# Modulation by VectorE multiply-and-sum in a two-layer hybrid backbone: shift and scale of the first layer in the filter stage, the rest beside the short convolutions

## The chip, the cores and the metric

One core of a Trainium2 chip runs the whole program. The metric is the device time of one execution in microseconds (us), the median of several runs. Engines are named as in the profile: TensorE (PE, weight loads PEld), VectorE (DVE), ScalarE (ACT), GpSimd (POOL) and SyncE (SP), which here only issues DMAs. Each engine works through its own instructions in order and waits on semaphores; a DMA is issued by an engine's queue, and an issue that stands behind a wait comes after it.

## The reference

Two layers are applied to 128 context tokens and 1024 latent tokens (1152 columns in all), 1024 channels wide. What the change touches is the modulation; it depends on the conditioning vectors alone (one for the context tokens, one for the latent tokens):

```python
mod = jax.nn.silu(cond) @ p['w_ada'] + p['b_ada']
shift, scale, gate = jnp.split(mod[:, None, :], 3, axis=-1)
h = rms_norm(x, p['norm_g']) * (1.0 + scale) + shift
proj = h @ p['w_in']
# three branches: long convolution (Hyena), differential attention, pooling
out = merged @ p['w_out']
return x + gate * out, kv
```

`w_ada` is 1024 x 3072 a layer, f32. Before the layers the spectra of the Hyena filters are computed: a small sine network gives filter taps, they are multiplied by a decay, normalised, and transformed.

## The kernel before

All tensors lie with channels on the 128 partitions; 1024 channels are KD = 8 tiles. Products of f32 numbers are made of three matmuls with operands split into a rounded high part and a rest, so each weight tile goes through ScalarE (rounding, `high`) and GpSimd or VectorE (the rest, `low`).

`filters` (phase "fspec", the first 566 us) has a head and four units. In the head TensorE runs the sine network (lines 434 and 451; VectorE reduces the angles in `reduce_and_sin`, lines 221 to 226; ScalarE takes the sine, line 714; VectorE makes the remainder of the last hidden layer, line 566), SP copies the hidden layer to the other partitions (lines 380 and 384), and for each of CT = 4 channel tiles and two directions TensorE makes the taps (`hidden_to_taps`, line 467) and VectorE multiplies them by the decay (`decayed`, line 578). GpSimd adds and subtracts directions (`both_of`, lines 695 and 696), VectorE folds (line 597), TensorE turns the folds (`turn`, line 486), ScalarE and VectorE split them (lines 747 and 605). ScalarE also squares x (line 727), GpSimd sums the squares (line 703) and TensorE sums over channels (line 526). Then four units (layer x order) of NS = 17 steps each: at a step SP stores the last spectrum tile (`store_spectrum`, lines 351 to 356; lines 353 and 354 are two stores of one tile) and loads the transform matrix of two steps later (`load_matrix`, line 339), ScalarE rounds that matrix (`matrix_high`, line 758) and copies the spectrum out (line 764), VectorE makes the matrix's rest (`matrix_low`, line 625), TensorE multiplies (line 514). In the same steps the taps of the next unit are made.

The modulation of both layers stands in `filters`, too. 48 tiles (24 a layer) of `w_ada`, 512 KB each, are loaded by SP into three buffers (`load_ada`, line 344) and multiplied on TensorE (`modulation`, line 443: KD matmuls of 128x128 weights by two columns a tile): five tiles in the sine network, eight before the taps, eight between the turns, seven in each unit from step 6 on. VectorE adds the bias (line 633).

Then a loop over the layers: `keys_values`, `attention`, `mixers_in`, `long_conv`, `branches_out`, `output`. `mixers_in` (phase "mixin") projects 28 tiles (`proj`, line 1292). SP loads the weight of tile t+2 in its step t (`load_w`, line 1224; from tile 3 on, and two buffers). ScalarE's order in step t is: round the weight of tile t+2 (`high`, line 1330), evict tile t (lines 1339 to 1341), issue two table copies. GpSimd makes the weight's rest (line 1399). For the first T_PL = 12 tiles VectorE runs the short convolution (lines 1416 to 1426), and SP stores it one step later, from tile 4 on (`store_conv`, lines 1240 and 1241). Four pooling tiles and twelve gating tiles follow. The next lines are SP's and ScalarE's loops before:

```python
for t in range(T_END):                       # SP
    if 3 <= t + 2 < T_END:
        load_w(t + 2) if t >= 1 else None
    ...
    if CT <= t - 1 < T_PL:
        store_conv(t - 1)
for t in range(T_END):                       # ScalarE
    if t + 2 < T_END:
        high(t + 2)
    if t < T_PL:
        evict_hy(t)
```

## Time and profile before

| | us |
|---|---|
| median of three runs | 3848.51 (3844.27 to 3859.57) |
| the profiled execution's own time | 3852.03 |
| its span in the trace | 3850.1 |
| TensorE busy in the span | 3500.3 |
| VectorE / ScalarE / GpSimd busy | 1654.7 / 1106.5 / 795.7 |
| mean granted TensorE clock | 0.941 of full |

A busy TensorE is not one at its peak: matmuls are pipelined and their ends are modelled. The rows below are instructions or groups of them with their line in the kernel; "idle" is the time that the engine stood still before, with what ended it.

### The profile page before, as it was taken

How to read it: one execution, taken by the hardware profiler on the slowest of the kernel's cores; microseconds unless marked ns; L12 is line 12 of the kernel's file. 1: busy time of each engine (PE TensorE's matmuls, PEld its weight loads, DVE VectorE, ACT ScalarE, POOL GpSimd, SP SyncE). 2: the span in 40 equal slices, each digit the busy share in tenths (PEclk: the TensorE clock that was granted, in tenths of full speed). 3: DMA queues.
4: the chain of work that ended last, by engine and by line, in shares of the span. 5: the costliest groups of instructions: out<-in, count | busy, mean ns of one | idle time of the engine just before them, and what ended most of it. 6: DMA issues, size and time to landing. Idle time of an engine off the chain costs nothing. (4 is left out here: it accounts for less than half of the span.)

```text
span 3850.1 us, 49480 instructions
## 1 busy us (share of the span) xinstructions
PE 3500.3 (91%) x19198; PEld 3255.1 (85%) x19198; DVE 1654.7 (43%) x2065; ACT 1106.5 (29%) x1765; POOL 795.7 (21%) x393
## 2 busy tenths in 40 slices
PE   5889888989999999988888889999999999888889
PEld 5777768988998999986788879889888999866889
DVE  2344524254454334237734132444544342377351
ACT  1233424243344312112211142334443112122111
POOL 2222202122122111112212322121221111122123
PEclk7688989999999999999999989999999999989999
DMA  5455553332332245346543433322322454456334
GB/s 173 149 176 178 164 194 124 123 84 68 82 85 63 83 151 185 139 160 206 194 152 119 163 142 125 86 62 79 91 63 77 142 185 142 156 199 218 134 119 168
DMA packets 212192, 520.14 MB, mean 135 GB/s; under 512 B 37012, under 2 KB 84757, under 8 KB 210614
## 3 DMA queue, kind: packets, MB, share of 16 engines
q1 hardware_dynamic: 203030, 458.56, 36.0%
q10 hardware_dynamic: 8960, 58.73, 5.0%
q8 instruction: 146, 2.39, 0.3%
q14 instruction: 56, 0.46, 0.0%
HBM read 381.19 MB, written 163.07 MB: 141 GB/s over the span
## 5 line engine op out<-in xcount | busy, mean ns | idle before, releaser
L2053 PE MATMUL ps<-hh,w_high 128*128 128x384 f32 x1152 | 413.2, 359 | 5.5 <-ACT attn_fout L2204 4.4
L2053 PE MATMUL ps<-hh,w_low 128*128 128x384 f32 x1152 | 393.9, 342 | 0.0
L2053 PE MATMUL ps<-hl,w_high 128*128 128x384 f32 x1152 | 392.4, 341 | 0.0
L1292 PE MATMUL ps<-hh,w_high 128*128 128x384 f32 x1344 | 310.7, 339 | 7.2 <-PEq L116 7.2
L1292 PE MATMUL ps<-hl,w_high 128*128 128x384 f32 x1344 | 306.7, 336 | 0.0
L1292 PE MATMUL ps<-hh,w_low 128*128 128x384 f32 x1344 | 306.4, 335 | 0.0
L2363 DVE TENSOR_REDUCE attn_nmax<-ps 128x1 f32<-128x1280 f32 x144 | 195.4, 1357 | 145.6 <-PE ps L2076 145.5
L1292 PEld LDWEIGHTS ps<-hh,w_high 128*128 128x128 f32 x1344 | 240.3, 189 | 11.6 <-POOLq L1396 7.8
L2230 ACT ACTIVATE low<-ps,attn_nmax 128x1280 f32<-128x1280 f32 x144 | 176.3, 1224 | 236.6 <-DVE attn_nmax L2363 236.6
L2383 DVE TENSOR_TENSOR attn_wl<-ps,attn_wh 128x512 fp32r<-128x512 f32 (+2 forms) x200 | 117.4, 587 | 290.1 <-ACT attn_wh L2240 290.1
L1292 PEld LDWEIGHTS ps<-hl,w_high 128*128 128x128 f32 x1344 | 240.9, 189 | 0.0
L1292 PEld LDWEIGHTS ps<-hh,w_low 128*128 128x128 f32 x1344 | 240.8, 189 | 0.0
L2053 PEld LDWEIGHTS ps<-hh,w_high 128*128 128x128 f32 x1152 | 222.2, 193 | 11.5 <-ACT attn_fout L2204 9.2
L2053 PEld LDWEIGHTS ps<-hl,w_high 128*128 128x128 f32 x1152 | 222.0, 193 | 0.0
L2053 PEld LDWEIGHTS ps<-hh,w_low 128*128 128x128 f32 x1152 | 220.9, 192 | 0.0
L2300 POOL TENSOR_TENSOR w_low<-w_raw,w_high 128x1024 fp32r<-128x1024 f32 x48 | 119.0, 2480 | 475.2 <-ACT w_high L2197 475.2
L2509 PE MATMUL ps<-hh,branch_wh 128*128 128x384 f32 x576 | 138.1, 349 | 41.9 <-POOL branch_wl L2552 41.9
L1737 POOL TENSOR_TENSOR conv_prod<-conv_prod 128x512 f32<-128x512 f32 x64 | 100.8, 1595 | 313.3 <-DVE conv_prod L1746 313.3
L1456 DVE TENSOR_TENSOR mixin_zg<-mixin_zg,mixin_yin 128x1152 f32<-128x1152 f32 x24 | 55.6, 2318 | 227.3 <-ACT mixin_zg L1358 227.3
L443 PEld LDWEIGHTS ps<-fspec_scond,fspec_araw 128*128 128x128 f32 x768 | 122.5, 249 | 35.4 <-DMA fspec_araw<-in_w_ada 31.5
L443 PE MATMUL ps<-fspec_scond,fspec_araw 128*128 128x2 f32 x768 | 119.4, 288 | 31.3 <-DMA fspec_araw<-in_w_ada 31.3
L2509 PEld LDWEIGHTS ps<-hh,branch_wh 128*128 128x128 f32 x576 | 106.4, 196 | 46.9 <-POOL branch_wl L2552 46.9
(289 smaller groups left out, 7548.8 us busy)
## 6 DMA issues: line engine op xcount, KB each, us to landing
tables<-in_dft_conv ACTq DMA_DIRECT2D x64, 512.0 KB, 4.4
gates<-attn_fout SPq DMA_DIRECT2D x144, 192.0 KB, 2.0
branch_gate<-gates SPq DMA_DIRECT2D x48, 576.0 KB, 3.9
H_dram<-fspec_hout SPq DMA_DIRECT2D x100, 256.0 KB
fspec_araw<-in_w_ada SPq DMA_DIRECT2D x48, 512.0 KB, 4.2
w_raw<-in_w_mg ACTq DMA_DIRECT2D x48, 512.0 KB, 3.9
conv_dh<-tables SPq DMA_DIRECT2D x96, 256.0 KB, 2.9
conv_dl<-tables SPq DMA_DIRECT2D x96, 256.0 KB, 3.6
```

Source lines behind the costliest of these rows:

```text
L443: last = pe.matmul(ps[:, 5, 2 * i:2 * i + 2], araw[:, i % 3, k, :], scond[:, k, :], start=(k == 0), stop=(k == KD - 1))
L1292: last = pe.matmul(dst, w[:, b, k, :], x[:, k, cols], start=(k == 0 and n == 0), stop=(k == KD - 1 and n == 2))
L1456: dve.tensor_tensor(zg[:, i % 2], zg[:, i % 2], yin[:, i % 2], ALU.mult).then_inc(S["gated"], 1)
L1737: pool.tensor_tensor(prod[:, p % 2, 2 * b], prod[:, p % 2, 2 * b], prod[:, p % 2, 2 * b + 1], (ALU.subtract, ALU.add)[b]).then_inc(S["gp"], 1)
L2053: last = pe.matmul(ps[:, X_BANK, 0:CH], w[:, j % 2, k, :], x[:, k, (c % 3) * CH:(c % 3 + 1) * CH], start=(k == 0 and n == 0), stop=(k == K ...
L2230: nc.scalar.activation(dst[:, 0:n], flat[:, 1536 * c:1536 * c + n], ACT.Exp, bias=nmax[:, c:c + 1], accum_out=total[:, u % 2, c:c + 1]).th ...
L2300: pool.tensor_tensor(fwl[:, b], fraw[:], fwh[:, b].bitcast(F32), ALU.subtract).then_inc(S["flo"], 1)
L2363: dve.tensor_reduce(nmax[:, c:c + 1], flat[:, 1536 * c:1536 * c + n], AX_X, ALU.max, negate=True).then_inc(S["max"], 1)
L2383: dve.tensor_tensor(weights(wl, u, at, cnt), ps[:, T_BANK, 0:cnt * P].rearrange("p (k c) -> p k c", c=P), weights(wh, u, at, cnt).bitcast( ...
L2509: last = pe.matmul(dst, w[:, b, k, :], x[:, q, cols], start=(k == 0 and n == 0), stop=(k == CT - 1 and n == 2))
```

## The change

TensorE's matmuls for the modulation go, with the bias loads of `filters`. `w_ada` is laid out by rows of output channels (128 partitions x 1024), and the conditioning vectors, after the Silu, are spread over all partitions. One output tile is then two VectorE instructions (`tensor_tensor_reduce`, one per vector): multiply 1024 elements by the vector and sum along the row. The 16 tiles of shift and scale of the first layer run in the head of `filters`; their loads (`w_ada_first`) are spread over SP's queue there. The other 24 of each layer's pass (the gate of this layer, shift and scale of the next) run in `mixers_in`, two behind each short convolution, with two load buffers that are the pooling's later. The bias is added where the values are used. The spread vectors are stored to DRAM once (`cond_kept`) and loaded back in `mixers_in`.

x's tiles are loaded earlier, six at once and two when a buffer is free, each with its own semaphore; ScalarE squares each on arrival, between the sines, and GpSimd's sums go into the first. The second store of a spectrum tile (line 354) goes; the first then counts for both.

```diff
@@ filters, SyncE
                 def load_ada(i):
                     if i >= 3:
-                        sp.wait_ge(S["a_used"], i - 2)
-                    sp.dma_start(araw[:, i % 3], A["w_ada"][i // 24, i % 24]).then_inc(s_ain[i % 3], 16)
+                        sp.wait_ge(S["ada"], 2 * (i - 2))
+                    sp.dma_start(araw[:, i % 3], A["w_ada_first"][i]).then_inc(s_ain[i % 3], 16)
+                def load_x(k):
+                    if k >= 6:
+                        sp.wait_ge(S["xadd"], k - 5)
+                    sp.dma_start(xs[k], A["x"][:, k]).then_inc(s_xin[k], 16)
...
-                        sp.dma_start(H_dram[l, o, t // 2, :, 0, :], src).then_inc(sem, 16)
-                        sp.dma_start(H_dram[l, o, t // 2, :, 2, :], src).then_inc(sem, 16)
+                        sp.dma_start(H_dram[l, o, t // 2, :, 0, :], src).then_inc(sem, 32)
...
-                sp.dma_start(cond[:], A["cond"]).then_inc(S["cond"], 16)
-                for i in range(3):
+                sp.dma_start(condb, A["cond"].to_broadcast([P, 2, D_MODEL])).then_inc(S["cond"], 16)
+                for i in range(2):
                     load_ada(i)
+                for k in range(6):
+                    load_x(k)
+                load_ada(2)
...
+                sp.wait_ge(S["scond"], 1)
+                sp.dma_start(cond_kept, condb).then_inc(S["cst"], 16)
+                for k in range(6, KD):
+                    load_x(k)
+                for i in range(3, 5):
                     load_ada(i)
...
-                for i in range(9, 14):
+                for i in range(5, 9):
                     load_ada(i)
                 for u in range(2, CT):
                     load_decay(u)
-                for i in range(14, ADA_AHEAD):
+                    for i in range(9 + 2 * (u - 2), 11 + 2 * (u - 2)):
+                        load_ada(i)
+                for i in range(13, NA):
                     load_ada(i)
@@ filters, TensorE
-                def modulation(i):
...
-                        last = pe.matmul(ps[:, 5, 2 * i:2 * i + 2], araw[:, i % 3, k, :], scond[:, k, :],
-                                         start=(k == 0), stop=(k == KD - 1))
...
+                pe.wait_ge(S["xadd"], KD - 1)
+                for i in range(NT // P):
+                    last = pe.matmul(ps[:, 5, i:i + 1], xs[0][:, i * P:(i + 1) * P], ones[:, 0:1], start=True, stop=True)
+                last.then_inc(S["ssm"], 1)
                 pe.wait_ge(S["dup"], 96)
@@ filters, VectorE
+                def modulation(i):
+                    if i == 0:
+                        dve.wait_ge(S["scond"], 1)
+                    dve.wait_ge(s_ain[i % 3], 16 * (i // 3) + 16)
+                    for st in range(2):
+                        if 2 * i + st:
+                            dve.wait_ge(S["ada"], 2 * i + st)
+                        dve.tensor_tensor_reduce(waste, araw[:, i % 3], condb[:, st], 1.0, 0.0, ALU.mult, ALU.add,
+                                                 modn[:, i, st:st + 1]).then_inc(S["ada"], 1)
+                for i in range(2):
+                    modulation(i)
                 dve.wait_ge(S["pre"], 2)
...
+                for i in range(2, 6):
+                    modulation(i)
                 for m in range(2):
                     matrix_low(m)
                 for ct in range(CT):
                     for d in range(2):
                         decayed(0, ct, d)
+                        modulation(6 + 2 * ct + d)
+                for i in range(14, NA):
+                    modulation(i)
@@ filters, GpSimd and ScalarE
                     if u == CT - 1:
-                        pool.wait_ge(S["ssm"], 1)
+                        pool.wait_ge(S["ada"], 2 * NA)
+                        pool.wait_ge(S["cst"], 16)
...
+                squares((0, 1))
                 for i in range(2):
+                    if i == 1:
+                        squares((2, 3, 4))
                     act.wait_ge(S["ang"], i + 1)
                     nc.scalar.activation((h1, h2)[i], ang, ACT.Sin).then_inc(S["sin"], 1)
...
+                squares((5, 6, 7))
...
+                    if m == 0:
+                        act.wait_ge(S["ada"], 2 * NA)
...
-                            act.wait_ge(S["a_used"], min(NA, ADA_AHEAD + ADA * n))
+                            if n:
+                                act.wait_ge(S["hpst"], 16 * n)
@@ keys_values, VectorE
-                chain(dve.tensor_copy(mod[:], mods[:, bass.ds(l, 1)].rearrange("p a m n -> p (a m) n")))
                 dve.wait_ge(S["par"], 16)
+                for st in range(2):
+                    chain(dve.tensor_tensor(mod[:, 0:2 * KD, st], modn[:, :, st], pr("b_ada")[:, 0:2 * KD], ALU.add))
@@ mixers_in, SyncE
+                def load_ada(i):
+                    if i >= 2:
+                        sp.wait_ge(S["ada"], 2 * (i - 1))
+                    sp.dma_start(araw[:, i % 2], A["w_ada"][l, i]).then_inc(s_ain[i % 2], 16)
                 load_w(2)
+                sp.dma_start(condb, cond_kept).then_inc(S["cond"], 16)
+                for i in range(2):
+                    load_ada(i)
...
                 for t in range(T_END):
                     if 3 <= t + 2 < T_END:
                         load_w(t + 2) if t >= 1 else None
+                    for i in (2 * t + 2, 2 * t + 3):
+                        if i < NA:
+                            load_ada(i)
@@ mixers_in, ScalarE and VectorE
                 def pool_out(g):
                     act.wait_ge(S["pmm"], 2 * g + 1)
+                    if g == 0:
+                        act.wait_ge(S["ada"], 2 * NA)
...
+                def modulation(i):
...
+                    for st in range(2):
...
+                        dst = mod[:, 2 * KD + i, st:st + 1] if i < KD else modn[:, i - KD, st:st + 1]
+                        dve.tensor_tensor_reduce(waste, araw[:, i % 2], condb[:, st], 1.0, 0.0, ALU.mult, ALU.add, dst
+                                                 ).then_inc(S["ada"], 1)
...
+                    for i in (2 * t, 2 * t + 1):
+                        modulation(i)
+                dve.wait_ge(S["ada"], 2 * NA)
+                for st in range(2):
+                    at = mod[:, 2 * KD:3 * KD, st]
+                    dve.tensor_tensor(at, at, pr("b_ada")[:, 2 * KD:3 * KD], ALU.add).then_inc(S["bada"], 1)
```

## Rows read from the trace of the kernel before

**Rows 1.** Page: TensorE's busy time; two groups (count | busy, mean ns | idle).

```profile
PE 3500.3 (91%) x19198; PEld 3255.1 (85%) x19198; DVE 1654.7 (43%) x2065; ACT 1106.5 (29%) x1765; POOL 795.7 (21%) x393
...
L2363 DVE TENSOR_REDUCE attn_nmax<-ps 128x1 f32<-128x1280 f32 x144 | 195.4, 1357 | 145.6 <-PE ps L2076 145.5
...
L443 PE MATMUL ps<-fspec_scond,fspec_araw 128*128 128x2 f32 x768 | 119.4, 288 | 31.3 <-DMA fspec_araw<-in_w_ada 31.3
```

**Rows 2.** Windows of line 443 alone: stretch, length, PE, PEld, clock, DMA share, GB/s.

```profile
122.00:167.00 45.00, 27.38 (x128) 27.67 (x128) 0.50 0.61 206
...
167.00:565.00 398.00, 50.00 (x432) 52.81 (x432) 0.90 0.52 171
```

**Rows 3.** Timeline of ScalarE, last unit: start, duration, instruction [idle before, ended by].

```profile
506.13 0.62 ACT L758 CAST fspec_dh<-fspec_draw 128x512 fp32r<-128x512 f32 x1 [2.88 <-DMA fspec_draw<-in_dft_taps]
...
514.15 0.62 ACT L758 CAST fspec_dh<-fspec_draw 128x512 fp32r<-128x512 f32 x1 [6.42 <-DMA fspec_draw<-in_dft_taps]
...
547.65 0.62 ACT L758 CAST fspec_dh<-fspec_draw 128x512 fp32r<-128x512 f32 x1 [3.83 <-DMA fspec_draw<-in_dft_taps]
...
551.95 0.62 ACT L758 CAST fspec_dh<-fspec_draw 128x512 fp32r<-128x512 f32 x1 [3.20 <-DMA fspec_draw<-in_dft_taps]
...
556.88 0.62 ACT L758 CAST fspec_dh<-fspec_draw 128x512 fp32r<-128x512 f32 x1 [3.83 <-DMA fspec_draw<-in_dft_taps]
```

**Rows 4.** Timeline of SyncE's queue, last unit.

```profile
503.70 1.34 SPq L344 DMA_DIRECT2D fspec_araw<-in_w_ada  x3
```

**Rows 5.** Timeline of ScalarE in `mixers_in` of the first layer.

```profile
1357.09 1.05 ACT L1330 CAST w_high<-w_raw 128x1024 fp32r<-128x1024 f32 x1 [10.29 <-PE ps L1292]
...
1358.99 0.28 ACT L1341 COPY aux<-ps 128x128 f32<-128x128 f32 x1
1369.57 1.05 ACT L1330 CAST w_high<-mixin_raw 128x1024 fp32r<-128x1024 f32 x1 [10.30 <-PE ps L1292]
```

**Rows 6.** Timelines of the head, all engines; last row VectorE in the first unit.

```profile
48.02 1.48 DVE L221 TENSOR_SCALAR fspec_both<-ps,fspec_fpar 128x1152 f32<-128x1152 f32 x1 [26.54 <-PE ps L451]
...
56.09 1.16 ACT L714 ACTIVATE fspec_both<-fspec_both 128x1152 f32<-128x1152 f32 x1 [33.41 <-DVE fspec_both L226]
...
60.67 1.36 DVE L566 TENSOR_TENSOR fspec_h2l<-fspec_both,fspec_h2h 128x1152 fp32r<-128x1152 f32 x1
61.58 11.48 POOL L703 TENSOR_TENSOR fspec_both<-fspec_both,fspec_taps 128x1152 f32<-128x1152 f32 x4 [61.12 <-ACT fspec_taps L727]
...
68.36 5.25 DVE L625 TENSOR_TENSOR fspec_dl<-fspec_draw,fspec_dh 128x512 fp32r<-128x512 f32 x2 [6.33 <-ACT fspec_dh L758]
...
70.18 0.60 SPq L384 DMA_DIRECT2D fspec_h2l<-fspec_h2l  x1
...
92.31 1.36 DVE L578 TENSOR_TENSOR fspec_taps<-ps,fspec_decay 128x1152 f32<-128x1152 f32 x1 [18.70 <-PE ps L467]
...
169.38 0.69 DVE L625 TENSOR_TENSOR fspec_dl<-fspec_draw,fspec_dh 128x512 fp32r<-128x512 f32 x1 [4.95 <-ACT fspec_dh L758]
```

**Rows 7.** Timeline of TensorE: last turn of the head, first spectrum.

```profile
158.59 1.95 PE L486 MATMUL ps<-ident,fspec_fold 128*128 128x128 f32 x8
...
162.82 2.07 PE L511 MATMUL ps<-fspec_mid,fspec_sgn 1*128 1x512 f32 x2 [0.78 <-DVE fspec_mid L610]
```

**Rows 8.** Timeline of VectorE in `mixers_in`: a convolution's end; a 128x1024 operation.

```profile
1363.93 0.35 DVE L1422 SCALAR_TENSOR_TENSOR low<-aux,mixin_cw 128x128 f32<-128x128 f32 x1
...
1594.32 1.21 DVE L1865 TENSOR_TENSOR aux<-low 128x1024 f32<-128x1024 f32 x1
```

**Rows 9.** Line 1224, the weight loads of `mixers_in`: time from issue to landing.

```profile
DMA to landing us min/median/max: 3.5/4.1/6.8
```

**Rows 10.** Timeline of SyncE's queue in `mixers_in`: a convolution's store, the next weight load.

```profile
1401.62 0.35 SPq L1240 DMA_DIRECT2D mix<-aux  x1
...
1402.63 0.65 SPq L1224 DMA_DIRECT2D mixin_raw<-in_w_mix  x1
```

**Rows 11.** Timeline of GpSimd in `mixers_in`.

```profile
1358.22 2.40 POOL L1399 TENSOR_TENSOR w_low<-w_raw,w_high 128x1024 fp32r<-128x1024 f32 x1 [10.07 <-ACT w_high L1330]
```

More of the change, by code:

```diff
@@ L198, in build @@
                     with nc.sbuf_tensor("w_raw1", [P, KD, P], F32) as raw1:
-                        keys_values(nc, A, O, l, ps, par, pr, mods, mod, ident, ones, sums, x_state, hh, hl, low, qraw, kraw,
+                        keys_values(nc, A, O, l, ps, par, pr, modn, mod, ident, ones, sums, x_state, hh, hl, low, qraw, kraw,
                                     craw, (fraw, raw1), fwh, fwl, lam, gain, qk, vrows)
@@ L301, in even_groups @@
             return [(j // 3, 2 * (j % 3)) for j in range(GA) if 9 + j // 2 == s]
-        def modulations(n, s):
-            i = ADA_AHEAD + n * ADA + s - 6
-            return [i] if 6 <= s < 6 + ADA and i < NA else []
         def odd_groups(s):
@@ L404, in _ @@
                             load_matrix(m + 2)
-                        if s == 4:
-                            sp.wait_ge(S["hpst"], 16 * (n + 1))
-                        for i in range(NA):
-                            if (s == 4 and i in sum((modulations(n, q) for q in (6, 7, 8)), [])) or (
-                                    s >= 6 and i in modulations(n, s + 3)):
-                                load_ada(i)
                         if n + 1 < NU and s in (3, 5, 7, 9):
@@ L523, in _ @@
                         hidden_to_taps(0, ct, d)
-                pe.wait_ge(S["xadd"], KD - 1)
-                for i in range(NT // P):
-                    last = pe.matmul(ps[:, 5, 128 + i:129 + i], xs[-1][:, i * P:(i + 1) * P], ones[:, 0:1], start=True,
-                                     stop=True)
-                last.then_inc(S["ssm"], 1)
                 for ct in range(CT):
-                    for i in (13 + 2 * ct, 14 + 2 * ct):
-                        modulation(i)
                     for f in (0, 2, 4):
@@ L538, in _ @@
                             prompt_spectrum(n)
-                        for i in modulations(n, s):
-                            modulation(i)
                         for ct, f in odd_groups(s):
@@ L792, in _, with keys_values @@
                                 high_part(n + 1, ct, f)
-def keys_values(nc, A, O, l, ps, par, pr, mods, mod, ident, ones, sums, x_state, hh, hl, low, qraw, kraw, craw, raws,
+def keys_values(nc, A, O, l, ps, par, pr, modn, mod, ident, ones, sums, x_state, hh, hl, low, qraw, kraw, craw, raws,
                 fwh, fwl, lam, gain, qk, vrows):
@@ L1179, with mixers_in @@
 T_PL, T_Z, T_END = 12, 16, 28
-def mixers_in(nc, A, l, ps, pr, hh, hl, v, aux, fold, fraw, fwh, fwl, mix, tables):
+def mixers_in(nc, A, l, ps, pr, mod, modn, cond_kept, hh, hl, v, aux, fold, fraw, fwh, fwl, mix, tables):
     with phase(nc, "mixin") as ph:
@@ L1200, in mixers_in @@
                  "pst0", "pst1", "y0", "y1", "gated", "zst0", "zst1", "dve", "tab",
-                 "fold")
+                 "fold", "cond", "ain0", "ain1", "ada", "bada")
         S = {n: ph.sem(n) for n in names}
@@ L2845, in lay_out @@
     A["w_out"] = _tiles(I["w_out"])
-    A["w_ada"] = _tiles(I["w_ada"])
-    A["cond"] = np.stack([I["c_ctx"], I["c"][0]]).reshape(2, KD, P).transpose(2, 1, 0)
+    ada = I["w_ada"].transpose(0, 2, 1).reshape(DEPTH, 3 * KD, P, D_MODEL)
+    A["w_ada_first"] = ada[0, 0:2 * KD]
+    A["w_ada"] = np.stack([np.concatenate([ada[l, 2 * KD:], ada[min(l + 1, DEPTH - 1), 0:2 * KD]]) for l in range(DEPTH)])
+    A["cond"] = np.stack([I["c_ctx"], I["c"][0]])[None]
     conv = np.concatenate([I["hy_conv_w"], I["hy_conv_b"][:, None]], axis=1)
```

87 lines of the change are left out of this document (38 added, 49 removed).

## The prediction

> **What bounds the kernel now.** Read the page first: TensorE is called busy for 91% of the span [rows 1], which invites the thought that any matmul taken off it is time gained. The modulation's 768 matmuls (line 443) stand there with 119.4 us busy and 31.3 us of idle time before them, which ended with a weight load. The windows of line 443 alone show where they lie: 27.4 us at half clock (0.50) in the stretch 122 to 167 us, 50.0 us in the four spectrum units from 167 to 565 us [rows 2]; the rest lies before 122 us. So nothing after 565 us can win. Three stretches decide, each with its own bound.
>
> The spectrum units are not bound by TensorE. Before each rounding of a transform matrix ScalarE is waiting for the matrix's DMA; near the end, where no modulation is left, the roundings still come 4.30 and 4.93 us apart by turns [rows 3]. That is a loop: rounding, spectrum copied out (the next instruction on ScalarE), store and next load on SP's queue, landing. The longer turn is the one with two stores. Where three ada tiles of 512 KB are issued at 503.70 [rows 4], the loop takes 8.02 us (506.13 to 514.15, idle until the DMA) [rows 3]: the tiles delay the matrix behind them.
>
> The head of the filter stage is a chain through all engines; its matmuls wait for ada DMAs. In `mixers_in`, where the new work goes, TensorE is the bound: ScalarE's weight rounding at line 1330 follows TensorE, 12.48 us a tile (1357.09 to 1369.57) [rows 5].
>
> **The change part by part.**
>
> *Head, to the first tap.* Now: the second angle is ready at 56.0, its remainder ends at 62.0 (60.67 + 1.36), the first taps start at 92.31, the first spectrum at 162.82 [rows 6, 7]. The wait for ada tiles ahead of the second layer's matmuls goes. New on that path: two squarings before the first sine (they wait for x 0 and 1, queued behind 2 MB of cond and ada, so about 1 to 2 us late), then four VectorE multiply-sums. No row shows such an instruction. The nearest is a plain 128x1024 two-input operation, 1.21 us [rows 8], 1.24 with a semaphore between; I take 1.24. Below that nothing is likely, since it reads the same elements; above, a multiply and a separate sum would be 1.21 + 1024/1280 x 1.36 (the reduction's row [rows 1]) = 2.3. Four take 5 us, beside the second layer's matmuls; the second reduction takes 8.1 (48.02 to 56.09) [rows 6]. GpSimd's sums of x squared (four in 11.48) move from after this chain into it. That costs: two VectorE splits that take 0.69 each at other times took 5.25 together beside these sums [rows 6]. With two or three sums of 2.87 in the way the second angle comes at 42 (36 without, 45 with all), the remainder at 48: 14 us earlier.
>
> Behind it SP copies the hidden layer as now (last copy issued at 70.18, 8 us after the remainder [rows 6], landing later), then loads ada tile 5, on which VectorE waits with the matrix splits and the first taps queued behind; and the three last sums, the x sums on TensorE and six multiply-sums share that time. I put the first taps at 68 against 92.3: 24 us gained.
>
> *Head, taps to spectrum.* Now 70.5 us (92.31 to 162.82). Then: eight taps of 1.36 with two multiply-sums each are 30.7; four multiply-sums more, 5.0; GpSimd's six fold sums in between hold VectorE up by about 12; the last fold sums wait for all multiply-sums (their buffer holds cond) and cost up to 5.3 beside VectorE's folds; then four groups of folds and turns without the two modulations each, 5.0 a group (0.8 for a fold, 4.2 from the turn at 158.59 to the spectrum at 162.82 [rows 7]), 20. Together 68 to 73; TensorE's 27.4 us give little, since VectorE takes their place. **Head: 27 us gained** (18 if the sums block more, 42 if they hardly block).
>
> *Spectrum units.* The gain is in the loop, not in the 50 us of matmuls. (a) The second store is dropped: 4.93 becomes 4.30, 0.63 x 8 a unit x 4 = 20. (b) The three tiles together: 8.02 becomes 4.9 with its own double store counted above, 3.4 x 4 = 14; the single tiles later about 1.5 us a unit, 6. **40 us gained**; 30 if TensorE at the lower clock sets some steps, 50 if the shorter steps also free waits for the folds.
>
> *Layer stage.* In `keys_values` a copy becomes two small additions: under 0.5 us a layer, hidden behind the load of `par`.
>
> *`mixers_in`.* 24 pairs of multiply-sums a layer, two pairs behind each of 12 short convolutions. VectorE has room: 4 x 1.24 = 5.0 in a tile of 12.48. But the 24 loads go on SP's queue, two a tile, with two buffers; the second waits for the multiply-sums of the same tile. Behind that wait stand the stores of the convolution and `load_w` of the next step (tile t+3); ScalarE waits for this weight in `high` **ahead of** the eviction of its own tile; the convolution waits for the eviction. A loop, then, priced from the start h of `high`:
> - h to evicted: 1358.99 + 0.28 - 1357.09 = 2.2 [rows 5];
> - convolution to 1363.93 + 0.35 = 1364.28: h + 7.2 [rows 5, 8];
> - multiply-sums: h + 12.2; ada issue and wake 0.5;
> - the weight: 4.1 issue to landing as median now, 3.5 to 6.8 [rows 9], and one ada tile of the same size straight ahead of it: 4.6;
> - ScalarE's wake 0.1.
>
> That is 17.4 a tile against 12.48. From the sixth on two stores go ahead (1401.62 to 1402.63, 1.0 [rows 10], and their bytes): 18.7. Eleven tiles pass through the loop: 5 x 17.4 + 6 x 18.7 = 199 against 11 x 12.48 = 137, 62 more. TensorE has 12.48 - 3.6 = 8.9 us of cover (the next but one tile needs `high` 1.05 and GpSimd's 2.40 after h [rows 5, 11]), once. **53 us lost a layer, 106 in two.** Bounds: landing 3.5 with nothing ahead gives 16.2 and 17.1, 37 a layer; 6.8 gives 19.5 and 20.4, 74 a layer. I take the middle since the ada tile is surely ahead. A lower clock after TensorE's waits hides in them.
>
> Sum: 3852.0 (profiled execution) - 27 - 40 + 106 = 3891. The median shown is 3.5 below the profiled execution: **3887.5**.
>
> *Put at nothing.* The 1 MB store of cond is issued some 17 us after the start and waited for near 110. x's loads pass ada tile 2, w3 and the decays, none of which VectorE or TensorE needs before 28 us; the last two x loads wait on GpSimd's first sums with ada 3 and 4 behind them, needed some 15 us later. ScalarE's new waits (all multiply-sums before the first spectrum copy, the prompt store before its buffer is written again) are met earlier by a stage or a unit. In `mixers_in` the pool's copy waits for all multiply-sums, done two tiles before; without that cover it would cost one eviction. The bias additions are two small instructions.
>
> *A rule against it.* Each multiply-sum reads two f32 tensors in SBUF and sums at once. The Trainium skill, "Vector Engine (DVE) Microarchitecture Reference", section 7, warns that one family of instructions that can accumulate halves its throughput with two such sources, as no port is left for the accumulator. No run here shows such a sum; the plain two-source form takes 1.21 us for 1024 elements, so some 1.2 ns an element with its fixed part [rows 8]. What a half rate would give is priced, from rows, as the second rival.
>
> **Rivals.**
> 1. *The loop is covered* (other side: faster). If weights land before TensorE needs them, only the head and the units count: 3848.5 - 67 = 3781.5. It decides where multiply-sums, issue and landing fit into 12.48 - 7.2 = 5.3 us; 5.0 + 0.5 + 4.6 = 10.1 speaks against it, as does the order in the code. For it: nothing in the rows but VectorE's idle time. A weaker form, larger gains (92) with the cheap loop (75), gives 3831.5.
> 2. *The multiply-sum takes 2.3 us*, a multiply plus a sum. In the loop 4 x 1.06 = 4.2 more a tile, 47 a layer, 94 in two; in the head some 25: 3887.5 + 119 = 4006. For it: nothing shows the fused form; against: a reduction alone also runs at an element per 1.06 ns.
> 3. *The two sides meet*: gains near 85 against losses near 85, 3848.5. The head is the weakest sum of all, its chain has five engines.
>
> **How the numbers follow.** A measurement of this kernel tells about 0.5% (19 us) from no change. Forecast with its bounds, beyond 0.5% slower: 0.60; rival 2: 0.07; rival 3, within 0.5%: 0.20; rival 1 in both forms, as far as it is beyond 0.5%: 0.13. So faster 0.13, same 0.20, slower 0.67. Range: gains 92 with losses 75 give 3831; gains 42 with losses 148 give 3954.5. Rounded, 3830 to 3960: below it lies most of rival 1, above it rival 2.
>
> **What would show it.** Right: the rows of line 1330 in `mixers_in` some 17 to 19 us apart in the first twelve tiles and 12.5 after, ended by a DMA instead of TensorE, TensorE idle before line 1292 by some 50 us a layer; the stage after the filters starting near 500 instead of 566; even and odd matrix roundings both near 4.3. Wrong: line 1330 still ended by TensorE at 12.5 (rival 1); multiply-sums of 2 us or more (rival 2); first spectrum later than 145 or earlier than 120 (the head).

## The result and the profile after

The median went from 3850.51 us (four runs) to **3911.37 us** (four runs), a ratio of 1.0166 with a 95% interval of 1.0146 to 1.0186: slower by 60.9 us. The forecast was 3887.5 us, 39 above the median then shown, within 3830 to 3960. The profiled execution took 3909.5 us, its span 3907.8.

Cut at the same instructions in both traces (first spectrum matmul, last matrix rounding, first instruction of ScalarE in each later stage), the spans compare so:

| stretch | before, us | after, us | difference | forecast |
|---|---|---|---|---|
| head, to the first spectrum | 162.82 | 134.80 | -28.0 | -27 |
| four spectrum units, to the last rounding | 394.06 | 357.57 | -36.5 | -40 |
| keys, values and attention, layer 1 | 773.4 | 775.3 | +1.9 | 0 |
| `mixers_in` and long convolution, layer 1 | 575.2 | 638.0 | **+62.8** | +53 |
| `mixers_in` and long convolution, layer 2 | 576.6 | 637.3 | **+60.7** | +53 |
| everything else | 1368.0 | 1364.8 | -3.2 | 0 |
| span | 3850.1 | 3907.8 | +57.7 | +39 |

The long convolution is not where it lies: in the first layer the last roundings of `mixers_in` stand 61 us further from its first one than before (1267.67 to 1663.24 against 1330.25 to 1664.53).

The timeline of ScalarE in `mixers_in` of the first layer, after (start, duration, instruction, idle before and what ended it). These rows answer [rows 5]; line 1330 is now line 1347:

```profile
1336.18 1.05 ACT L1347 CAST w_high<-w_raw 128x1024 fp32r<-128x1024 f32 x1 [16.08 <-DMA w_raw<-in_w_mix]
...
1338.09 0.28 ACT L1358 COPY aux<-ps 128x128 f32<-128x128 f32 x1
1353.46 1.05 ACT L1347 CAST w_high<-mixin_raw 128x1024 fp32r<-128x1024 f32 x1 [15.10 <-DMA mixin_raw<-in_w_mix]
...
1370.41 1.05 ACT L1347 CAST w_high<-w_raw 128x1024 fp32r<-128x1024 f32 x1 [14.76 <-DMA w_raw<-in_w_mix]
...
1389.67 1.05 ACT L1347 CAST w_high<-mixin_raw 128x1024 fp32r<-128x1024 f32 x1 [17.08 <-DMA mixin_raw<-in_w_mix]
...
1409.32 1.05 ACT L1347 CAST w_high<-w_raw 128x1024 fp32r<-128x1024 f32 x1 [17.46 <-DMA w_raw<-in_w_mix]
```

A rounding that TensorE used to end every 12.48 us is ended by the weight's DMA, first some 17.5 us apart and later 19 to 20. VectorE, and SyncE's queue, in the same tiles (x2: two issues in the time given, with the wait between them):

```profile
1338.40 1.86 DVE L1447 TENSOR_SCALAR aux<-aux,mixin_cw 128x1154 f32<-128x1154 f32 x1 [8.27 <-ACT aux L1358]
...
1342.95 0.35 DVE L1453 SCALAR_TENSOR_TENSOR low<-aux,mixin_cw 128x128 f32<-128x128 f32 x1
1343.22 1.22 DVE L1437 CUSTOM_DVE_ANT_0 mixin_diff<-mixin_grow,mixin_pout 128x1024 f32<-128x1024 f32 x1
...
1347.12 1.23 DVE L1437 CUSTOM_DVE_ANT_0 mixin_diff<-mixin_grow,mixin_pout 128x1024 f32<-128x1024 f32 x1
```

```profile
1345.88 2.98 SPq L1260 DMA_DIRECT2D mixin_grow<-in_w_ada  x2
1349.04 0.33 SPq L1230 DMA_DIRECT2D mixin_raw<-in_w_mix  x1
...
1399.24 2.98 SPq L1260 DMA_DIRECT2D mixin_grow<-in_w_ada  x2
1402.27 1.13 SPq L1246 DMA_DIRECT2D mix<-aux  x1
1403.44 0.43 SPq L1247 DMA_DIRECT2D mix<-aux  x1
1404.06 0.81 SPq L1230 DMA_DIRECT2D w_raw<-in_w_mix  x1
```

Read across the three: eviction ends at 1338.37, the convolution at 1343.30, the fourth multiply-sum at 1348.35, and 0.7 us later the weight is issued whose landing lets ScalarE go on at 1353.46. From the sixth tile on the two stores lie between the last ada issue and the weight.

What TensorE loses to it, in two groups of all instructions (count | busy, mean ns | idle before), and what a multiply-sum costs (the profile calls it a custom instruction) in `mixers_in` and in the head:

```profile
L1309 PE MATMUL ps<-hh,w_high 128*128 128x384 f32 x1344 | 326.5, 352 | 91.0 <-POOL w_low L1418 83.8
...
L1437 DVE CUSTOM_DVE_ANT_0 mixin_diff<-mixin_grow,mixin_pout 128x1024 f32<-128x1024 f32 x96 | 117.5, 1224 | 5.1
...
L544 DVE CUSTOM_DVE_ANT_0 fspec_hout<-fspec_araw,fspec_both 128x1024 f32<-128x1024 f32 x32 | 58.7, 1835 | 3.2 <-DMA fspec_araw<-in_w_ada_first 1.9
```

The projection (line 1309, before 1292) now stands idle for 83.8 us until the weight's rest is there, and its three groups are busy for 960.4 us instead of 923.8: 120 us together, close to the 123.5 us that both layers lose. The head, in VectorE's and then TensorE's timeline, answers [rows 6, 7]; the roundings of the last unit answer [rows 3]:

```profile
26.23 3.48 DVE L544 CUSTOM_DVE_ANT_0 fspec_hout<-fspec_araw,fspec_both 128x1024 f32<-128x1024 f32 x1
...
41.35 0.76 DVE L227 TENSOR_SCALAR fspec_both<-fspec_both 128x1152 f32<-128x1152 f32 x1
...
46.73 3.69 DVE L559 TENSOR_TENSOR fspec_h2l<-fspec_both,fspec_h2h 128x1152 fp32r<-128x1152 f32 x1
...
68.33 1.35 DVE L571 TENSOR_TENSOR fspec_taps<-ps,fspec_decay 128x1152 f32<-128x1152 f32 x1
```

```profile
134.80 2.07 PE L497 MATMUL ps<-fspec_mid,fspec_sgn 1*128 1x512 f32 x2 [0.77 <-DVE fspec_mid L603]
```

```profile
483.69 0.62 ACT L757 CAST fspec_dh<-fspec_draw 128x512 fp32r<-128x512 f32 x1 [3.21 <-DMA fspec_draw<-in_dft_taps]
488.08 0.62 ACT L757 CAST fspec_dh<-fspec_draw 128x512 fp32r<-128x512 f32 x1 [3.29 <-DMA fspec_draw<-in_dft_taps]
492.37 0.62 ACT L757 CAST fspec_dh<-fspec_draw 128x512 fp32r<-128x512 f32 x1 [3.18 <-DMA fspec_draw<-in_dft_taps]
```

### The profile page after: what moved, and what is told of

It is laid out like the page before. It is cut to its first block and busy times, and to the rows that moved or that the text cites. A ratio compares the mean times of both kernels' runs of the same rounds, so it can differ in the third digit from the quotient of the medians.

```text
span 3907.8 us, 48339 instructions
## 1 busy us (share of the span) xinstructions
PE 3423.0 (88%) x18430; PEld 3170.0 (81%) x18430; DVE 1835.4 (47%) x2323; ACT 1109.0 (28%) x1765; POOL 805.0 (21%) x393
## 5 line engine op out<-in xcount | busy, mean ns | idle before, releaser
L2090 PE MATMUL ps<-hh,w_high 128*128 128x384 f32 x1152 | 414.6, 360 | 5.5 <-ACT attn_fout L2241 4.4
L1309 PE MATMUL ps<-hh,w_high 128*128 128x384 f32 x1344 | 326.5, 352 | 91.0 <-POOL w_low L1418 83.8
L2090 PE MATMUL ps<-hh,w_low 128*128 128x384 f32 x1152 | 395.0, 343 | 0.0
L2090 PE MATMUL ps<-hl,w_high 128*128 128x384 f32 x1152 | 393.6, 342 | 0.0
L1309 PEld LDWEIGHTS ps<-hh,w_high 128*128 128x128 f32 x1344 | 250.2, 197 | 101.8 <-POOL w_low L1418 90.2
L1309 PE MATMUL ps<-hl,w_high 128*128 128x384 f32 x1344 | 318.2, 346 | 0.0
L1309 PE MATMUL ps<-hh,w_low 128*128 128x384 f32 x1344 | 315.7, 343 | 0.0
L1309 PEld LDWEIGHTS ps<-hl,w_high 128*128 128x128 f32 x1344 | 251.9, 197 | 0.0
L1309 PEld LDWEIGHTS ps<-hh,w_low 128*128 128x128 f32 x1344 | 250.2, 196 | 0.0
L2090 PEld LDWEIGHTS ps<-hh,w_high 128*128 128x128 f32 x1152 | 222.7, 193 | 11.7 <-ACT attn_fout L2241 9.2
L2090 PEld LDWEIGHTS ps<-hl,w_high 128*128 128x128 f32 x1152 | 223.0, 194 | 0.0
L2090 PEld LDWEIGHTS ps<-hh,w_low 128*128 128x128 f32 x1152 | 221.8, 193 | 0.0
L1447 DVE TENSOR_SCALAR aux<-aux,mixin_cw 128x1154 f32<-128x1154 f32 x24 | 44.8, 1868 | 216.3 <-ACT aux L1358 216.3
L2241 ACT ACTIVATE attn_fout<-ps 128x384 f32<-128x384 f32 x144 | 71.0, 493 | 256.6 <-PE ps L2090 256.6
```

Source lines behind the costliest of these rows:

```text
L1309: last = pe.matmul(dst, w[:, b, k, :], x[:, k, cols], start=(k == 0 and n == 0), stop=(k == KD - 1 and n == 2))
L1447: chain(dve.tensor_scalar(dst, u[:, b, 1:1 + n], taps[:, 1:2], taps[:, 3:4], ALU.mult, ALU.add))
L2090: last = pe.matmul(ps[:, X_BANK, 0:CH], w[:, j % 2, k, :], x[:, k, (c % 3) * CH:(c % 3 + 1) * CH], start=(k == 0 and n == 0), stop=(k == K ...
L2241: nc.scalar.activation(fout[:, c % 2], ps[:, X_BANK, 0:CH], ACT.Tanh, scale=0.5).then_inc(S["fev"], 1)
```

## The experiments

The theory on record: the weight load in `mixers_in` stands on SyncE's queue behind a wait for the multiply-sums, and ScalarE's order closes that into a loop; the units gain what leaves their loop on the same queue, not TensorE's work; the head gains by the waits for ada tiles. Where one run is given (no interval), the verdict rests on its trace: stretches that an edit does not touch differ by up to 9 us from one execution to the next (the four units took 352.1 to 361.1 us in the changed kernel and the six variants of it that leave them alone).

**Is it the queue's order?** In `mixers_in` of the changed kernel:

```diff
 for t in range(T_END):                       # SP
-    if 3 <= t + 2 < T_END:
-        load_w(t + 2) if t >= 1 else None
+    if t + 3 < T_END:
+        load_w(t + 3)
     for i in (2 * t + 2, 2 * t + 3):
         if i < NA:
             load_ada(i)
```

> The changed kernel with one order turned round on SyncE's queue in mixers_in: at step t the weight of tile t+3 is issued ahead of the two ada tiles instead of behind them; same instructions, same loads. Theory (the weight load stands behind a wait for the multiply-sums, a loop of 17.4 to 20 us): the weight roundings in the first twelve tiles come 12.5 us apart and end with TensorE, the layer stage gets back 61 us a layer, 3911 - 122 = 3789 us, 62 below the kernel before. Rival A (the multiply-sums or the added traffic themselves stretch the tiles): roundings stay 16 us or more apart, 3890 to 3911. Rival B (another wait takes the place, the ada tiles land too late for VectorE and the evictions wait for it): roundings 13 to 15 us apart, 3810 to 3860.

Measured: 3813.25 us against 3847.09 for the kernel before, ratio 0.991 (0.9886 to 0.9933): 98 us back by an order alone, but not 122. ScalarE's timeline shows where the rest is, and VectorE's and SyncE's show why:

```profile
1354.67 1.05 ACT L1347 CAST w_high<-mixin_raw 128x1024 fp32r<-128x1024 f32 x1 [10.29 <-PE ps L1309]
1367.15 1.06 ACT L1347 CAST w_high<-w_raw 128x1024 fp32r<-128x1024 f32 x1 [10.29 <-PE ps L1309]
...
1380.92 1.06 ACT L1347 CAST w_high<-mixin_raw 128x1024 fp32r<-128x1024 f32 x1 [11.58 <-DMA mixin_raw<-in_w_mix]
...
1397.98 1.06 ACT L1347 CAST w_high<-w_raw 128x1024 fp32r<-128x1024 f32 x1 [14.87 <-DMA w_raw<-in_w_mix]
```

```profile
1351.84 2.98 SPq L1260 DMA_DIRECT2D mixin_grow<-in_w_ada  x2
1354.86 0.43 SPq L1246 DMA_DIRECT2D mix<-aux  x1
```

```profile
1363.01 0.88 DVE L1447 TENSOR_SCALAR aux<-aux,mixin_cw 128x1154 f32<-128x1154 f32 x1 [8.70 <-DMA mix<-aux]
```

Seven steps of 12.48 us, ended by TensorE: the first loop is gone. Then the convolution of tile 6 waits 8.7 us for the store of tile 4 (each convolution from the seventh on needs the store of two tiles back to have landed), and that store was issued at 1354.86, behind the two ada tiles, that is behind the multiply-sums of tile 5. A **second loop through the same queue**, 17 us a tile, which the first had covered. From there on one VectorE instruction a tile also runs beside GpSimd's rest of a weight and takes 3.2 to 3.6 us instead of 1.2 to 1.4 (the convolution's last one, 1382.13 to 1385.67). My expectation had not seen this loop; rival B's time (3810 to 3860) holds, but not its steps (13 to 15), and the wait that took the place is the store's and not an ada tile's.

**Another link of the same loop cut**, SyncE's order as in the changed kernel:

```diff
 for t in range(T_END):                       # ScalarE
+    if t < T_PL:
+        evict_hy(t)
     if t + 2 < T_END:
         high(t + 2)
     if t < T_PL:
-        evict_hy(t)
+        pass
```

> The changed kernel with another link of the same loop cut, SyncE's order left as it is: in mixers_in ScalarE evicts tile t of the first twelve before it rounds the weight of tile t+2. Theory: the convolution no longer waits for a weight; the weight of t+3 is issued 10.5 us after the eviction of t, lands 4.6 later, is split 3.6 later, 18.8 in all against some 23 until TensorE needs it: roundings 12.5 us apart, 3789 to 3810 us. Rival A (traffic or VectorE's work): roundings stay 16 us or more apart, 3890 to 3911.

```profile
1366.30 0.88 DVE L1449 TENSOR_SCALAR aux<-aux,mixin_cw 128x1154 f32<-128x1154 f32 x1 [6.22 <-DMA mix<-aux]
```

Measured: 3837.80 us, one run. Roundings 12.1 to 13.0 us apart from the third to the seventh (1303.30, 1315.82, 1328.27, 1340.38, 1353.37), then 14 to 18.5, where the convolution waits for a store. The same two pictures as in e1, by a cut elsewhere: the first loop needs ScalarE's order as much as SyncE's. The time expected was missed through the second loop in the main. A layer's stretch with `mixers_in` is still 10 us longer than in e1 (599.1 and 600.8 us against 588.6 and 591.8): here the weight stays behind the multiply-sums, the roundings wait for it from the third on, and the step ahead of that takes 16.6 us; the rest of the 10 was not followed up.

**More work in the loop**, each multiply-sum of `mixers_in` twice (the counts in the waits for them are doubled too):

```diff
-                    for st in range(2):
-                        if 2 * i + st:
-                            dve.wait_ge(S["ada"], 2 * i + st)
+                    for r in range(4):
+                        st = r % 2
+                        if 4 * i + r:
+                            dve.wait_ge(S["ada"], 4 * i + r)
...
```

> The changed kernel with each multiply-sum of mixers_in done twice into the same place (four more of 1.24 us a tile, 5.0). Theory: every link of the loop adds to it, so the roundings come 22.4 us apart in the first six tiles and 24.4 after, 11 x 5.0 = 55 us a layer more, 4021 us. Rival A (the traffic sets the step): the added VectorE work fits into its idle time, under 20 us more.

```profile
1366.05 1.05 ACT L1347 CAST w_high<-mixin_raw 128x1024 fp32r<-128x1024 f32 x1 [19.86 <-DMA mixin_raw<-in_w_mix]
1388.45 1.05 ACT L1347 CAST w_high<-w_raw 128x1024 fp32r<-128x1024 f32 x1 [20.21 <-DMA w_raw<-in_w_mix]
1412.70 1.05 ACT L1347 CAST w_high<-mixin_raw 128x1024 fp32r<-128x1024 f32 x1 [22.07 <-DMA mixin_raw<-in_w_mix]
```

Measured: 4012.68 us. The first five steps of the loop mean 22.3 us (17.5 in the changed kernel), the next six 24.5 (19.5): 4.8 and 5.0 us for 5.0 us of added work. VectorE's work counts in full while it stands in the loop, though in the changed kernel VectorE is idle for 7 to 10 us of each of these steps. The time is 101 us above the changed kernel's (110 expected; the rival allowed 20).

**Both loops cut.** As e1, and the stores go ahead of the ada tiles too:

```diff
+    if CT <= t - 1 < T_PL:
+        store_conv(t - 1)
     for i in (2 * t + 2, 2 * t + 3):
         ...
-    if CT <= t - 1 < T_PL:
-        store_conv(t - 1)
```

> As e1, and in mixers_in the two stores of convolution t-1 are issued ahead of the ada tiles of step t as well. In e1 the first seven tiles came 12.48 us apart and the next five about 17, where VectorE waits 5.9 to 8.7 us for the store of the convolution two tiles back, which stood behind the wait for the multiply-sums. Theory (a second loop through the same queue, hidden in the changed kernel behind the first): all roundings in mixers_in 12.5 us apart and ended by TensorE, 14 us a layer less than e1, 3813 - 28 = 3785 us, as much as the filter stage alone gains (64.5). Rival (from the sixth tile on traffic, not order, sets the step): steps of 16 to 17 stay, 3805 to 3815.

```profile
1366.48 1.05 ACT L1347 CAST w_high<-w_raw 128x1024 fp32r<-128x1024 f32 x1 [10.30 <-PE ps L1309]
1378.96 1.05 ACT L1347 CAST w_high<-mixin_raw 128x1024 fp32r<-128x1024 f32 x1 [10.30 <-PE ps L1309]
```

```profile
1363.65 3.00 SPq L1260 DMA_DIRECT2D mixin_grow<-in_w_ada  x2
1366.83 0.33 SPq L1230 DMA_DIRECT2D mixin_raw<-in_w_mix  x1
1367.20 0.68 SPq L1246 DMA_DIRECT2D mix<-aux  x1
```

Measured: **3783.04 us** against 3852.81, ratio 0.9822 (0.9806 to 0.9838). The first fourteen steps behind the first one are 12.48 us each, as in the kernel before; the two stretches with `mixers_in` take 576.2 us each, as in the kernel before (575.2 and 576.6). So the 96 multiply-sums and 48 ada loads cost nothing there: the whole loss was the order of issues on one queue.

**The units: stores, loads or matmuls?** Three edits of the kernel before. One store instead of two:

```diff
-                        sp.dma_start(H_dram[l, o, t // 2, :, 0, :], src).then_inc(sem, 16)
-                        sp.dma_start(H_dram[l, o, t // 2, :, 2, :], src).then_inc(sem, 16)
+                        sp.dma_start(H_dram[l, o, t // 2, :, 0, :], src).then_inc(sem, 32)
```

> The kernel before with the second store of a spectrum tile left away and nothing else changed. Theory (the store stands in the loop from rounding to rounding): even and odd roundings both 4.3 us apart where they were 4.30 and 4.93, the four units 20 us shorter, 3827 us. Rival (the second store is hidden by TensorE or by the next landing): within 5 us of the kernel before.

```profile
525.36 0.62 ACT L757 CAST fspec_dh<-fspec_draw 128x512 fp32r<-128x512 f32 x1 [3.20 <-DMA fspec_draw<-in_dft_taps]
529.55 0.62 ACT L757 CAST fspec_dh<-fspec_draw 128x512 fp32r<-128x512 f32 x1 [3.08 <-DMA fspec_draw<-in_dft_taps]
533.80 0.62 ACT L757 CAST fspec_dh<-fspec_draw 128x512 fp32r<-128x512 f32 x1 [3.15 <-DMA fspec_draw<-in_dft_taps]
```

Measured: 3825.33 us against 3852.81, ratio 0.9934 (0.9917 to 0.9951). Even and odd steps alike; the units 371.8 us (533.80 - 162.02) instead of 394.1, 22.3 less. The loads left out, 27 in SyncE's loop over the steps, and TensorE's wait for them (it waits for the prompt spectrum's copy instead):

```diff
-                        for i in range(NA):
-                            if (s == 4 and i in sum((modulations(n, q) for q in (6, 7, 8)), [])) or (
-                                    s >= 6 and i in modulations(n, s + 3)):
-                                load_ada(i)
...
-                    pe.wait_ge(s_ain[i % 3], 16 * (i // 3) + 16)
+                    if i < ADA_AHEAD:
+                        pe.wait_ge(s_ain[i % 3], 16 * (i // 3) + 16)
...
                         for i in modulations(n, s):
+                            pe.wait_ge(S["hpo"], n + 1)
```

> The kernel before with the 27 ada loads of the spectrum units left out; TensorE's matmuls on these tiles stay and read what lies in the buffers. Theory (the gain in the units is the loads' place on SyncE's queue, not TensorE's work): one step of 8.0 us a unit becomes 4.9, single tiles give 1.5 us a unit, 20 us in all, 3828 us. Rival (TensorE's 50 us of matmuls bound the units): no change.

Measured: units 382.4 us (542.57 - 160.22), 11.7 less, not much above the scatter of such stretches; the single run took 3835.26. The step with three tiles went from 8.4 us (196.29 to 204.68, three ada issues at 195.09) to 4.9 (193.00 to 197.91), as reckoned, but no gain by the single tiles shows. And the matmuls left out:

```diff
-                    for k in range(KD):
+                    nk = KD if i < ADA_AHEAD else 1
+                    for k in range(nk):
...
-                                         start=(k == 0), stop=(k == KD - 1))
+                                         start=(k == 0), stop=(k == nk - 1))
```

> The kernel before with seven of the eight matmuls left out for each ada tile of the spectrum units; all loads and waits stay. Theory: units as long as before within 5 us, 3843 to 3848 us. Rival (TensorE bounds the units): seven eighths of 50.0 us, 44 us less, 3803 us.

Measured: units 389.7 us (550.33 - 160.67), 4.4 less, which is within the scatter, where TensorE lost seven eighths of 50.0 us of work. The one run's 3833.01 is lower than that gives; the rest lies in stretches that the edit does not touch, none of them more than 5.2 us, and is not put down to it.

**The head: what do the sums of x squared cost?** In the changed kernel GpSimd's sums cut to a ninth (e7, the first edit), and in another kernel ScalarE's squares put back to their old place (e11, the second):

```diff
-pool.tensor_tensor(xs[0], xs[0], xs[k], ALU.add)
+pool.tensor_tensor(xs[0][:, 0:P], xs[0][:, 0:P], xs[k][:, 0:P], ALU.add)
```

```diff
-                squares((0, 1))
...
-                    if i == 1:
-                        squares((2, 3, 4))
...
-                squares((5, 6, 7))
+                squares(range(KD))
```

> The changed kernel with GpSimd's seven sums of x squared in the head cut from 1152 to 128 columns; the rest of these sums is left out, all waits stay. It prices the sums on arrival. Theory (they hold VectorE up where both work): second angle ready at 36 instead of 42, the split of the hidden layer and two multiply-sums at 1.3 instead of 3.6 us, first spectrum at 122 to 128 instead of 134.8, the whole run 7 to 12 us shorter than the changed kernel, 3900 us. Rival (the head hangs on the hidden layer's copies and the ada tiles, not on VectorE): first spectrum at 132 or later, no change in time.

```profile
125.15 2.07 PE L497 MATMUL ps<-fspec_mid,fspec_sgn 1*128 1x512 f32 x2 [0.78 <-DVE fspec_mid L603]
```

Measured: first spectrum at 125.15, 9.7 us earlier; second angle ready at 35.0; the third and fourth multiply-sum took 1.31 and 1.35 us instead of 3.48 and 3.51, the remainder 1.53 instead of 3.69. The single run's 3886.73 is lower than these 9.7 us give; the surplus stands in no one place.

> The changed kernel with one part undone: ScalarE squares x where it did before, all eight tiles after the hidden layer's rounding and w3, not on arrival. Theory (the sums hold VectorE up wherever they stand, so their place gives little): second angle ready at 36 to 37 instead of 42, but the sums then lie beside the remainder, the multiply-sums and the first taps; first spectrum within 3 us of 134.8. Rival A (squares on arrival are worth something): first spectrum 140 or later. Rival B (late is better): 130 or earlier.

Measured: second angle ready at 34.7, but five of the six multiply-sums behind the remainder then took 3.4 to 3.65 us beside the sums; first spectrum at 136.37, 1.6 us later than with the squares on arrival (3898.30 us, one run). The place of the squares is worth next to nothing; the sums cost VectorE the same anywhere.

**What the same reading is worth elsewhere.** The units had a loop of the same kind, so the matrix load was put ahead of the store that waits for ScalarE's copy, on top of e8:

```diff
-                        if m:
-                            store_spectrum(m - 1)
                         if m + 2 < NU * NS:
                             load_matrix(m + 2)
+                        if m:
+                            store_spectrum(m - 1)
```

> As e8, and in the spectrum units SyncE issues the matrix load of step m+2 ahead of the store of spectrum m-1, which waits for ScalarE's copy. The same kind of loop as in mixers_in: rounding, copy out, store, load, landing, 4.3 us a step. Theory: the load then hangs on VectorE's split of matrix m alone, and TensorE sets the step, 12 matmuls at 0.235 and a turn, 3.3 to 3.6 us; of 68 steps some 24 go by the taps (9 us a pair) and stay, some 40 gain 0.7 to 1.0: the units 25 to 40 us shorter, 3783 - 30 = 3753 us. Rival (something else, the landing or the folds, ends at nearly the same time): under 8 us.

```profile
438.67 0.62 ACT L757 CAST fspec_dh<-fspec_draw 128x512 fp32r<-128x512 f32 x1
441.86 0.62 ACT L757 CAST fspec_dh<-fspec_draw 128x512 fp32r<-128x512 f32 x1 [0.36 <-DMA fspec_draw<-in_dft_taps]
444.70 0.62 ACT L757 CAST fspec_dh<-fspec_draw 128x512 fp32r<-128x512 f32 x1 [0.49 <-DMA fspec_draw<-in_dft_taps]
```

Measured: **3744.24 us** against 3848.94, ratio 0.9723 (0.9707 to 0.9740), with the next one the fastest of all kernels here. Steps of 2.5 to 3.5 us where there were 4.3; the units 318.1 us instead of 358.8.

On top of it, the sums of x squared on TensorE:

```diff
-                pe.wait_ge(S["xadd"], KD - 1)
-                for i in range(NT // P):
-                    last = pe.matmul(ps[:, 5, i:i + 1], xs[0][:, i * P:(i + 1) * P], ones[:, 0:1], start=True, stop=True)
+                for k in range(KD):
+                    pe.wait_ge(S["xsq"], k + 1)
+                    for i in range(NT // P):
+                        last = pe.matmul(ps[:, 5, i:i + 1], xs[k][:, i * P:(i + 1) * P], ones[:, 0:1], start=(k == 0 and i == 0),
+                                         stop=(k == KD - 1 and i == NT // P - 1))
+                    if 0 < k < KD - 1:
+                        last.then_inc(S["xadd"], 1)
...
-                    pool.tensor_tensor(xs[0], xs[0], xs[k], ALU.add).then_inc(S["xadd"], 1)
```

> As e9, and GpSimd's sums of x squared go: TensorE sums all eight squared tiles over channels into one PSUM row group (72 matmuls of 128x1 instead of 9, in its idle time between the second layer and the taps). Theory (e7: the sums cost the head 9.7 us by holding VectorE up): second angle ready at 35, first spectrum at 125, 9 us less than e9. Rival (TensorE's 8 x 4.0 us end after the hidden layer's copies and delay the taps): the first taps later than 65 us, no gain or up to 5 us lost.

```profile
59.63 1.23 DVE L549 CUSTOM_DVE_ANT_0 fspec_hout<-fspec_araw,fspec_both 128x1024 f32<-128x1024 f32 x1 [6.53 <-DMA fspec_araw<-in_w_ada_first]
```

Measured: 3745.81 us, 1.6 above e9, no difference that these runs can tell. The second angle was ready at 35.0 and the first spectrum at 129.71 instead of 134.59, half of what was expected. VectorE's first tap came at 63.25, right behind the multiply-sums and splits that had waited for ada tile 5; in e7 that tile landed at 55.09. The hidden layer's first copies are issued alike (41.04 here, 41.24 in e7). But the loads of x 6 and 7, which wait for buffers that the sums free, come at 34.41 instead of 20.88, with ada tiles 3 and 4 behind them, just ahead of the copies; the copies that need the first ones landed come at 52.96 instead of 48.66, and ada tile 5 behind them. So the queue's order took the other half, by these rows; no run tests it. TensorE's sums, which ended at 57.4, were done before that tile landed. Where the 4.9 us went in the total is not settled.

Last, the kernel before with one store and with the matrix load ahead, its modulation left on TensorE (the diffs of e4 and e9):

> The kernel before with e9's order in the units (matrix load ahead of the spectrum store) and with one store a spectrum tile as in e4; the modulation stays on TensorE, the loads of ada in the units. It asks whether taking the modulation off TensorE is worth more once TensorE sets the step. Theory: it is; in e9 the four units take 318 us, here the 50.0 us of TensorE's modulation (rows of the kernel before) come back onto the path for the most part, 40 us: units 358 us, and with the head's 28 us the time is 3744 + 28 + 40 = 3812. Rival (the matmuls fit into what waits are left, as in e6; only the loads' place counts, 12 us as in e5): units 330 us, 3784.

Measured: 3803.78 us against 3846.92, ratio 0.9881 (0.9856 to 0.9906). Units 349.7 us (512.43 - 162.72) against 318.1 in e9: 31.6 us for the ada loads and matmuls that cost 11.7 and 4.4 in the kernel before. Nearer to the theory's 40 than to the rival's 12. TensorE is busy for 338.4 of these 349.7 us, against 358.4 of 394.1 in the kernel before: the work counts once TensorE sets the step. That it is the matmuls rather than the loads is argued from this, since no run takes away one of the two here.

## Why the prediction was right, step by step

**What bounds the kernel.** Three stretches, each with its own bound: shown by the table above; outside them the sum of all differences is -1.3 us. That TensorE's 50 us of matmuls in the units were next to no gain is shown by e6 (4.4 us for seven eighths of them).

**The loop in `mixers_in`** is shown by e1, e2 and e3: cut in two different links it vanishes in the first tiles, and work put into it comes out one for one. Its terms, for the rounding at 1336.18: evicted at h + 2.2 (reckoned 2.2), convolution done at h + 7.1 (7.2), multiply-sums at h + 12.2 (12.2), weight issued at h + 12.9 (12.7), landed and taken up at h + 17.3 (17.4). The first five steps mean 17.5.

**The step that was too small** is the loss of 53 us a layer; 62.8 and 60.7 were measured, so the forecast of +39 became +61. The term mis-sized most is the landing behind the stores. In the first layer the six steps from the sixth on mean 19.5 instead of 18.7. The stores took about what was reckoned: the weight is issued 13.8 us after the rounding on the mean (reckoned 13.7), though the two stores shown above are the longest of the six pairs (1.6 us; the others 0.9). From its issue to the next rounding the weight then needs 5.3 to 6.5 us, 5.7 on the mean (5.3 for the one shown, 1404.06 to 1409.32), where 5.0 was left in the 18.7. So 11 steps are 204.2 us, not 199. The step ahead of them took 15.4 instead of 14.4. And TensorE's cover gave back 6.6 us at the end (steps of 2.70 and 15.65 where 25 would stand), not 8.9. Together 8.5 us of the 7.7 to 9.8.

**The second loop** was overlooked. The prediction counted the stores as traffic ahead of the weight, not as something that the convolution waits for. It cost nothing in the changed kernel, whose first loop is longer: there every convolution from the second tile on waits 7.1 to 10.5 us for its eviction and none for a store. So it could not falsify the sum; it was 24 us of e1's expectation.

**Rivals.** The loop was not covered (rival 1): every rounding from the third to the thirteenth was ended by the DMA. The multiply-sum took 1.22 us, not 2.3 (rival 2): 1.24 had been taken from the plain two-input row [rows 8]. The Trainium skill, "Vector Engine (DVE) Microarchitecture Reference", section 7, warns of half the rate for one family of instructions that can sum, with two sources in SBUF that are not bf16; in this form the trace does not show it: 1224 ns a piece in `mixers_in`, and a read of the accumulator of 0.08 us behind each. Whether this instruction is one of the family the trace does not say; the measurement decides for it. The 2.3 us of rival 2 would have made the time 4006 us.

**Head.** 28.0 gained, 27 forecast. Second angle 42.1 (42), remainder done 50.4 (48), first taps 68.3 (68), first spectrum 134.8 (136). From the first taps to the spectrum it took 66.5 us, less than the 68 to 73 reckoned; the 27 had taken the low end of these. That the sums on GpSimd hold VectorE up is shown by e7, 9.7 us in all; e11 shows that their place, a part of the change, is worth 1.6.

**Units.** 36.5 gained, 40 forecast. The second store 22.3 (20 reckoned), the three tiles together about 3.5 a unit (3.4 reckoned), the single tiles nothing that shows (6 reckoned): e5 gives 11.7 for all loads. The parts measured alone, 22.3, 11.7 and 4.4, add up to 38.4; the last two are single runs, and such stretches scatter by up to 9 us.

**The range.** Its upper end, 3954.5, takes gains of 42 us, but the low ends stated for the two gains, 18 and 30, add up to 48; that would give 3948.5. The measured time lies inside either.

**Put at nothing.** The stores, loads and waits listed there left no trace in the table; the additions of the bias neither.

## What to carry to other kernels

A DMA issue that stands behind a wait makes every later issue of its queue wait too: for each new wait on a queue, list what stands behind it, who needs that, and whether that one feeds the wait. Work on an engine that is half idle is not free if it lies in such a loop, and it is free as soon as the issues that others need go ahead of it (+61 us and -70 us for the same instructions). When a loop is cut, look at once for the next one through the same queue.

## What the runs showed of the hardware

- VectorE and GpSimd, each with two operands in SBUF, took turns instead of running side by side: a multiply-sum of 1.22 us took 3.48 and 3.51 beside GpSimd's sums, and three of these took 9.73 us, 3.24 each, where a single one took 2.66. The Trainium skill, "SBUF — State Buffer", section "SBUF: two separate sides", says that the two engines share a port pair as an exclusive lock, so that the loser blocks for a whole instruction; the rows agree, and e7's 1.31 and 1.35 us with short GpSimd sums are the other half of it.
- After its waits TensorE ran at the lower of its two levels: the granted clock was 0.50 from 1339.70 to 1344.60, behind a wait, and 1.00 from 1346.30 on. This row is a window over a tile of the changed kernel (stretch, length, TensorE busy, granted clock, DMA share, GB/s); the rows under it are its matmuls in an earlier tile, after 5.47 us idle and 8 us later:

```profile
1409.32:1428.47 19.15, 14.46 (x72) 0.82 0.49 168
```

```profile
1339.70 1.33 PE L1309 MATMUL ps<-hh,w_high 128*128 128x384 f32 x3 [5.47 <-POOL w_low L1418]
...
1347.92 0.68 PE L1309 MATMUL ps<-hh,w_low 128*128 128x384 f32 x3
```

  Three matmuls that take 0.68 us at 2.4 GHz took 1.16 to 1.33 until 1344.67. That goes with the 36.6 us that the projection is busier, but it is no cause of the loss: the tile waited for its weight anyway, and in e8, without the waits, both are gone (922.5 us busy).
- A multiply with a sum over 1024 elements cost VectorE hardly more than the plain operation, 1.22 against 1.21 us [rows 8], with 0.08 us for the read of the sum behind it.
